# Modulation weights of the first block dealt out unit by unit between the linears of a two-block transformer kernel

## The chip, the cores and the metric

One Trainium2 chip, one of its NeuronCores. The time is that of one execution on the device in microseconds (us); of several executions the median is given. Beside it stands the profile of one execution.

## The reference

Two models run one after the other on 256 tokens of width 1024 (the second also on 256 context tokens), each two layers deep. Only the first matters here:

```python
for l in range(DEPTH):                        # DEPTH = 2
    mod = silu(c) @ w_mod[l] + b_mod[l]       # 1024 -> 6 x 1024, one vector
    sh1, sc1, g1, sh2, sc2, g2 = split(mod, 6)
    h = modulate(rms_norm(x, mix_norm_g[l]), sh1, sc1)
    x = x + g1 * token_mixer(h, ...)
    h = modulate(rms_norm(x, ffn_norm_g[l]), sh2, sc2)
    x = x + g2 * channel_mixer(h, ...)        # up, causal conv of 3 taps, silu(a) * b, down
```

The token mixer has three branches that a gate merges: attention from latents (q and k are expanded from normed latents by `w_uq` and `w_ukv`, head-normed and rotated), attention from a plain projection ("qkb", "vb"), and a gated depthwise convolution of 31 taps ("conv"). The modulation vector of a layer is six groups of 1024 numbers; a group needs 1024 x 1024 weights, 4 MB, for one vector. The second model's layers have nine groups for two vectors.

## The kernel before

**Weights.** All weights lie in one stream in the order of use, cut into units of eight 128x128 blocks (512 KB). SyncE loads unit u into slot u % 8 of `ring` (L499) as soon as TensorE has done with unit u - 8. `weight_blocks` writes the order out by hand; TensorE's code asks for the blocks in the same order.

**Split units.** Large matmuls are made in three passes of a faster format: ScalarE copies a landed unit into `heads` (L1148, four slots), VectorE writes the remainder into `rests` (L1537), and TensorE multiplies head by head, head by rest and rest by head (L577 to L579). Splits are placed into the programs of ScalarE and VectorE by `upcoming` (up to three split units and five units ahead of the unit that an event belongs to) or, in the FFNs, two behind each pair of output blocks. uq, uk, uv, pw2, oa, ob, out and the modulation weights aren't split; their matmuls are at L581, each in two entries of the trace.

**Modulation.** `mod_rows` on TensorE takes a group: unit k holds the weights of input block k for all 1024 outputs, two matmuls with 32 columns as stationary operand and 512 moving ones. They go to output partitions 32 * (2 * (k % 2) + r) for r = 0, 1 of one PSUM bank, so that an even and an odd unit use four different strips of the array. ScalarE copies the bank into `rows` (L1313), `mod_cols` on TensorE turns it into columns with eight entries of 2 or 4 moving columns, and VectorE adds the bias (L1551). A group whose matmuls are put between other work is called a guest.

**Order in a mixer.** lat (six units), guest group 2 as a whole, the squares' sums of the latents (ones-matmuls), uq, uk, uv, `mod_cols` of group 2 and guest group 3 as a whole (`hook`), then `head_norm` of q: for each of four pairs of heads a bank of head sums, behind it one pair of qkb output blocks (two units), then the rotation. `head_norm` of k likewise with the conv blocks. Then vb, `mod_cols` of group 3 and guest group 4 as a whole, the head sums of qkb's keys, three gate pairs (`early_gates`), and attention with five more. VectorE makes for each head pair a reciprocal of 128x512 (L1640) and a product (L1641), for each rotation three operations (L1653 to L1656); ScalarE the root ahead of the reciprocal (L1199, in `roots`). PSUM banks 0 to 5 go round: `take_bank` waits for whoever read the tenant before. ScalarE copies the four qkb banks (L1360, L1362, L1179) behind all four roots of q and the squares of k.

**Order in an FFN of the first block.** 22 pairs j of up-projection blocks, two units each (the first two pairs together as a quad), and behind pairs 3 and 4, 10 and 11, 17 and 18 four guest units each; `mod_cols` behind pairs 5, 12 and 19. Then the down-projection.

Two layers of mixer and FFN make up the first 1260 us or so.

## Time and profile before

| | |
|---|---|
| median of 3 runs | 2936.59 us (2926.67 to 2941.27) |
| profiled execution | 2939.55 us, span 2937.8 us |
| granted TensorE clock, mean | 0.970 of full speed |
| busy: TensorE, its weight loads, VectorE, ScalarE | 94%, 79%, 57%, 37% of the span |
| stream | 836 units of 512 KB, mean 152 GB/s |
| chain that ended last | TensorE 84%, VectorE 8%, DMA 3%, ScalarE 3% |

A row of the trace's timeline has the start, the length, the engine, the line, the tiles written and read, the shape and the number of instructions merged; in brackets the idle time of the engine before it and what ended it. PE is TensorE, DVE VectorE, ACT ScalarE. Ends of matmuls are modelled and overlap the next start a little.

### The profile page before, as it was taken

To read this page: it belongs to the slowest core of one execution; us is meant where nothing else is said; L and a number is where in the kernel's file an instruction comes from. 1 tells how busy PE (TensorE), PEld (TensorE's weight loads), DVE (VectorE), ACT (ScalarE), POOL (GpSimd) and SP (SyncE) were. 2 spreads that over 40 slices of the span, in tenths; PEclk is the share of its full clock that TensorE was granted. 3 is DMA by queue.
4 is the path that set the end of the run, shared out by engine and by line. 5 is a ranking of instruction groups with operands and counts; after the bars stand their busy time and mean duration, and the time that the engine had idled before them with its cause. 6 is when DMAs were issued, how large, how long until landed. Compare 5 with 4: busy or idle time off the path is not lost.

```text
span 2937.8 us, 38582 instructions
## 1 busy us (share of the span) xinstructions
PE 2761.8 (94%) x15792; PEld 2329.9 (79%) x15792; DVE 1661.9 (57%) x2417; ACT 1097.8 (37%) x1660; POOL 51.6 (2%) x54
## 2 busy tenths in 40 slices
PE   7898899998988989989999899999989999989998
PEld 4777788896777988977878784888877788878998
DVE  4689436753896366655555534564565554364554
ACT  3445325643454155533122322222233222234443
POOL 0000000000000000000000000000000000000000
PEclk8999999999999999999999999999999999999999
DMA  8451346656332557536454312444334543231453
GB/s 331 172 172 58 116 156 242 223 160 222 127 120 77 194 196 252 184 123 229 143 186 137 108 64 68 140 147 139 138 129 167 186 156 136 94 101 40 156 185 116
DMA packets 122753, 447.27 MB, mean 152 GB/s; under 512 B 13521, under 2 KB 14929, under 8 KB 122193
## 3 DMA queue, kind: packets, MB, share of 16 engines
q1 hardware_dynamic: 122576, 444.81, 44.3%
q8 instruction: 125, 2.05, 0.3%
q14 instruction: 52, 0.42, 0.0%
HBM read 443.71 MB, written 1.05 MB: 151 GB/s over the span
## 4 chain that ended last, share of the span: by engine, by line
PE 84%; DVE 8%; DMA 3%; ACT 3%; issue 1%; SPq 0%; ACTq 0%; DVEq 0%
PE ps L577 22%; PE ps L578 22%; PE ps L579 22%; PE ps L581 18%; DMA ring<-stream 3%; DVE area L1640 2%; DVE rests L1537 1%; DVE area L1844 1%; DVE rs L1600 1%; ACT heads L1148 1%; DVE area L1610 0%; DVE stat L1672 0%; DVE sg L1684 0%; DVE rt L1736 0%; DVE h_split L1618 0%
## 5 line engine op out<-in xcount | busy, mean ns | idle before, releaser
L577 PE MATMUL ps<-h_split,heads 128*128 128x256 f32 (+1 forms) x2992 | 1006.7, 336 | 99.5 <-DVE h_split L1618 57.2
L578 PE MATMUL ps<-h_split,heads 128*128 128x256 f32 (+1 forms) x2992 | 986.3, 330 | 0.0
L579 PE MATMUL ps<-h_split,rests 128*128 128x256 f32 (+1 forms) x2992 | 985.8, 329 | 0.0
L1537 DVE TENSOR_TENSOR rests<-ring,heads 128x1024 fp32r<-128x1024 f32 x520 | 631.1, 1231 | 362.1 <-ACT heads L1148 354.5
L1148 ACT ACTIVATE heads<-ring 128x1024 fp32r<-128x1024 f32 x520 | 536.9, 1056 | 594.6 <-PE ps L579 298.1
L577 PEld LDWEIGHTS ps<-h_split,heads 128*128 128x128 f32 x2992 | 588.3, 197 | 190.2 <-DVE h_split L1618 62.7
L578 PEld LDWEIGHTS ps<-h_split,heads 128*128 128x128 f32 x2992 | 588.4, 197 | 48.3 <-issue 4.3
L579 PEld LDWEIGHTS ps<-h_split,rests 128*128 128x128 f32 x2992 | 587.1, 196 | 46.1
L577 PE MATMUL ps<-hid_split,heads 128*128 128x256 f32 (+1 forms) x1056 | 355.2, 336 | 0.0
L579 PE MATMUL ps<-hid_split,rests 128*128 128x256 f32 (+1 forms) x1056 | 354.9, 336 | 0.0
L578 PE MATMUL ps<-hid_split,heads 128*128 128x256 f32 (+1 forms) x1056 | 354.9, 336 | 0.0
L1760 DVE TENSOR_TENSOR sg<-sg,ps 128x512 f32<-128x512 f32 (+1 forms) x88 | 54.7, 622 | 330.4 <-PE ps L579 284.6
L581 PE MATMUL ps<-area,ring 128*128 128x256 f32 (+1 forms) x800 | 210.0, 423 | 13.7 <-DVE area L1804 9.8
L1301 ACT ACTIVATE sg<-ps 128x512 f32<-128x512 f32 (+1 forms) x88 | 47.6, 541 | 458.8 <-PE ps L579 458.8
L578 PEld LDWEIGHTS ps<-hid_split,heads 128*128 128x128 f32 x1056 | 199.3, 189 | 20.7
L579 PEld LDWEIGHTS ps<-hid_split,rests 128*128 128x128 f32 x1056 | 199.3, 189 | 20.6
L577 PEld LDWEIGHTS ps<-hid_split,heads 128*128 128x128 f32 x1056 | 199.3, 189 | 20.3
L581 PEld LDWEIGHTS ps<-area,ring 128*128 128x128 f32 x800 | 155.1, 196 | 63.3 <-issue 40.4
L1630 DVE SCALAR_TENSOR_TENSOR x_sb<-ps,mods_sb,x_sb 128x256 f32<-128x256 f32 x160 | 71.9, 480 | 162.3 <-PE ps L581 85.1
L1574 DVE SCALAR_TENSOR_TENSOR qt<-ring,cols,qt 128x1024 f32<-128x1024 f32 x84 | 104.2, 1282 | 57.0 <-DMA ring<-stream 55.9
L1736 DVE SCALAR_TENSOR_TENSOR rt<-work,cols,rt 128x256 f32<-128x256 f32 x176 | 77.5, 482 | 51.3 <-ACT work L1251 49.7
L1844 DVE SCALAR_TENSOR_TENSOR area<-area,cols 128x256 f32<-128x256 f32 x240 | 100.2, 480 | 1.1
(180 smaller groups left out, 2226.1 us busy)
## 6 DMA issues: line engine op xcount, KB each, us to landing
ring<-stream SPq DMA_DIRECT2D x836, 512.0 KB, 3.8
consts<-constants SPq DMA_DIRECT2D x1, 1728.0 KB, 11.0
x_sb<-x_in SPq DMA_DIRECT2D x1, 1024.0 KB, 11.5
x_sb<-ctx_in SPq DMA_DIRECT2D x1, 1024.0 KB, 4.8
out<-area SPq DMA_DIRECT2D x1, 1024.0 KB, 4.8
consts<-constants SPq DMA_DIRECT2D x1, 576.0 KB, 8.9
cols<-columns SPq DMA_DIRECT2D x1, 538.0 KB, 9.9
cols<-columns SPq DMA_DIRECT2D x1, 157.5 KB, 2.4
```

The costliest lines, as they stand in the source:

```text
L577: nc.tensor.matmul(out, lhsT[0], rhs[0], start=first, stop=False)
L578: nc.tensor.matmul(out, lhsT[0], rhs[1], start=False, stop=False)
L579: ins = nc.tensor.matmul(out, lhsT[1], rhs[0], start=False, stop=last)
L581: ins = nc.tensor.matmul(out, lhsT, rhs, start=first, stop=last)
L1148: nc.scalar.activation(heads[:, n % HEADS_RING, :], ring[:, u % RING, :], ACT.Copy)\
L1537: nc.vector.tensor_tensor(rests[:, u % RING, :], ring[:, u % RING, :], as_f32(heads[:, n % HEADS_RING, :]), ALU.subtract)\
L1574: ins = nc.vector.scalar_tensor_tensor(out=half[:, v, :], in0=ring[:, u % RING, :], scalar=c, in1=half[:, v, :], op0=ALU.mult, op1=ALU.add)
L1630: nc.vector.scalar_tensor_tensor(out=x[:, v, m, :], in0=bank((p, *what, m))[:, t], scalar=gate(m, v), in1=x[:, v, m, :], op0=ALU.mult, op1 ...
L1640: step(nc.vector.reciprocal(b, b))
L1736: nc.vector.scalar_tensor_tensor(out=zc[:, s, ab, :], in0=z[:, s, ab, tap:tap + SEQ], scalar=cols[:, at:at + 1], in1=zc[:, s, ab, :], op0= ...
L1760: step(nc.vector.tensor_tensor(s_, s_, src, ALU.mult), (p, "gated", j))
L1844: nc.vector.scalar_tensor_tensor(out=dwc[:, c, :], in0=u_pad[:, c, tap:tap + SEQ], scalar=w, in1=dwc[:, c, :], op0=ALU.mult, op1=ALU.add)\
```

## The change

The eight units of a guest group are dealt out. In the first block's two FFNs each group goes over six successive pairs (units 0 and 1, 2, 3, 4 and 5, 6, 7), `mod_cols` behind the seventh; groups begin at pairs 0, 7 and 14. In a mixer three units of group 2 stand ahead of the latents' ones-matmuls and five behind; group 3 is spread over uq (2), uk (2) and the four qkb pairs (1 each), group 4 over the four conv pairs and the first four gate pairs. `mod_cols` of group 2 comes behind uq and that of group 3 ahead of the second conv pair; that of group 4 stays. ScalarE copies the first two qkb banks between the roots of q, and copies the rows of groups 3 and 4 later in its order. The stream's order follows. VectorE's order changes only with the pairs at which it adds an FFN group's bias. The second model's FFNs keep their places.

```diff
+def mixer_guests(l, stage, c):
+    _, second, third = MIXER_MODS[l]
+    if stage in ("uq", "uk"):
+        return second, [2 * (stage == "uk"), 2 * (stage == "uk") + 1]
+    if stage == "qkb":
+        return second, [4 + c]
+    if stage == "conv":
+        return third, [c]
+    return third, [4 + c] if c < 4 else []
...
+SPREAD = 6
...
 def guest_at(up, j):
     groups = FFN_MODS[up]
-    every = FJ // max(len(groups), 1)
+    if up in ("up_0", "up_1"):
+        q, at = divmod(j, SPREAD + 1)
+        if q < len(groups):
+            return groups[q], [k for k in range(KD) if k * SPREAD // KD == at]
+        return None, []
...
@@ the stream @@
         linear(f"uq_{l}", Q_RANK // P, range(HEADS))
+        guests(l, "uq")
         linear(f"uk_{l}", KV_RANK // P, range(HEADS))
+        guests(l, "uk")
         wide(f"uv_{l}", KV_RANK // P, 4)
-        mods(MIXER_MODS[l][1])
-        linear(f"qkb_{l}", KD, range(HEADS))
-        linear(f"conv_{l}", KD, range(2 * CC))
+        for stage in ("qkb", "conv"):
+            for c in range(4):
+                linear(f"{stage}_{l}", KD, (2 * c, 2 * c + 1))
+                guests(l, stage, c)
         wide(f"vb_{l}", KD, 4)
-        mods(*MIXER_MODS[l][2:])
         for m in range(KD):
             linear(f"gate0_{l}", KD, (m,))
             linear(f"gate1_{l}", KD, (m,))
+            guests(l, "gate", m)
...
@@ TensorE, mixer @@
-                hook(*guests[0])
+                mod_rows(*guests[0], range(3))
                 out = take_bank((p, "latms"))
...
+                mod_rows(*guests[0], range(3, KD))
...
+                mod_cols(*guests[0])
+                guests_behind("uq")
...
+                guests_behind("uk")
...
-                hook(*guests[1])
                 def pair_behind(what, name):
                     def do(c):
+                        if what == "conv" and c == 1:
+                            mod_cols(*guests[1])
                         out = take_bank((p, what, c))
                         linear(out[:, 0:SEQ], name, KD, 2 * c, hx)
                         linear(out[:, SEQ:TOK], name, KD, 2 * c + 1, hx, (p, what, c))
+                        guests_behind(what, c)
...
-                hook(*guests[2])
+                pending.append(guests[2])
...
@@ ScalarE, mixer @@
-                mod_rows(*guests[1])
-                roots((p, "qa"), range(4))
-                squares((p, "ka"), range(4), kt)
-                for c in range(2):
+                def second_copies(c):
                     act.wait_ge(tensor_done, after(T, (p, "qkb", c)))
+                    if c >= 2:
+                        copy_pair(pair_of(bt, c), (p, "qkb", c))
+                        return
...
-                for c in (2, 3):
-                    copy_pair(pair_of(bt, c), (p, "qkb", c))
+                roots((p, "qa"), range(4), between=second_copies)
+                squares((p, "ka"), range(4), kt)
+                second_copies(2)
+                second_copies(3)
+                mod_rows(*guests[1])
...
-                for guest in guests[2:]:
-                    mod_rows(*guest)
...
+                def gates_behind(t):
+                    if t % 3 == 2:
+                        early_gates(3 + t // 3)
+                    if t == 2:
+                        mod_rows(*guests[2])
```

## Rows read from the trace of the kernel before

**Rows 1.** The page: busy time, share of the span, instructions.
```profile
PE 2761.8 (94%) x15792; PEld 2329.9 (79%) x15792; DVE 1661.9 (57%) x2417; ACT 1097.8 (37%) x1660; POOL 51.6 (2%) x54
```
**Rows 2.** Stages of the first mixer: us, busy by engine, clock, DMA share, GB/s.
```profile
54.70:96.90 42.20, 37.31 (x175) 23.98 (x174) 5.95 (x7) 12.92 (x20) 0.00 (x0) 0.92 0.72 263
96.90:175.40 78.50, 66.41 (x423) 57.17 (x424) 73.29 (x64) 40.89 (x50) 0.00 (x0) 0.93 0.41 143
...
217.00:306.00 89.00, 79.76 (x542) 69.05 (x541) 83.91 (x227) 50.21 (x109) 0.00 (x0) 0.96 0.21 66
```
**Rows 3.** TensorE's waits in the first FFN (423 to 645): total, times, longest.
```profile
PE ps L577 <- DVE rests L1537: 7.3, 4, 2.5
...
PE ps L581 <- ACT rows L1313: 3.0, 3, 1.0
```
**Rows 4.** The same in the second FFN (1036 to 1257).
```profile
PE ps L577 <- DVE rests L1537: 6.3, 4, 2.3
...
PE ps L581 <- ACT rows L1313: 3.5, 3, 1.5
```
**Rows 5.** TensorE's timeline: lone unit, runs of eight, first entries behind waits.
```profile
15.38 1.05 PE L581 MATMUL ps<-ring,cols 128*32 128x512 f32 x4 [0.21 <-DMA ring<-stream]
...
54.70 4.63 PE L581 MATMUL ps<-ring,cols 128*32 128x512 f32 x32
...
66.57 13.79 PE L581 MATMUL ps<-area,ring 128*128 128x256 f32 x52 [4.88 <-DVE area L1804]
79.78 6.64 PE L581 MATMUL ps<-area,ring 128*128 128x256 f32 x30
...
90.56 4.42 PE L581 MATMUL ps<-ring,cols 128*32 128x512 f32 x32
94.91 1.98 PE L581 MATMUL ps<-sq,consts 128*128 128x512 f32 x4
...
121.00 0.58 PE L577 MATMUL ps<-h_split,heads 128*128 128x256 f32 x1 [4.49 <-ACT area L1362]
...
184.85 0.95 PE L581 MATMUL ps<-consts,rows 128*128 128x2 f32 x8
185.73 3.79 PE L581 MATMUL ps<-ring,cols 128*32 128x512 f32 x32
193.86 0.36 PE L577 MATMUL ps<-h_split,heads 128*128 128x256 f32 x1 [2.44 <-DVE rests L1537]
...
452.88 0.36 PE L577 MATMUL ps<-h_split,heads 128*128 128x256 f32 x1 [1.43 <-DVE rests L1537]
```
**Rows 6.** TensorE's timeline around a run of four units in an FFN.
```profile
500.00 0.28 PE L579 MATMUL ps<-h_split,rests 128*128 128x256 f32 x1
500.21 1.92 PE L581 MATMUL ps<-ring,cols 128*32 128x512 f32 x16
...
502.28 0.28 PE L578 MATMUL ps<-h_split,heads 128*128 128x256 f32 x1
```
**Rows 7.** VectorE's timeline: first reciprocals of the early and the late head norms.
```profile
102.03 3.35 DVE L1640 RECIPROCAL area<-area 128x512 f32<-128x512 f32 x1
...
197.62 3.35 DVE L1640 RECIPROCAL area<-area 128x512 f32<-128x512 f32 x1 [1.26 <-ACT area L1199]
```
**Rows 8.** ScalarE's timeline ahead of the roots of both head norms.
```profile
90.50 1.91 ACT L1354 ACTIVATE kt<-area 32x2048 f32<-32x2048 f32 x1
97.25 1.06 ACT L1148 ACTIVATE heads<-ring 128x1024 fp32r<-128x1024 f32 x1 [4.84 <-DMA ring<-stream]
98.51 1.06 ACT L1148 ACTIVATE heads<-ring 128x1024 fp32r<-128x1024 f32 x1 [0.20 <-DMA ring<-stream]
...
196.90 1.27 ACT L1199 ACTIVATE area<-ps,cols 128x512 f32<-128x512 f32 x2
```
**Rows 9.** TensorE in two stretches of 5 us: busy, clock, DMA share, GB/s.
```profile
470.00:475.00 5.00, 5.00 (x31) 0.66 0.19 77
475.00:480.00 5.00, 5.00 (x44) 1.00 0.64 212
```

More of the change, by code:

```diff
@@ L103, in guest_at @@
     groups = FFN_MODS[up]
-    every = FJ // max(len(groups), 1)
+    if up in ("up_0", "up_1"):
[3 more added lines that the diff above has]
+        return None, []
     for q, group in enumerate(groups):
-        first = GUEST_PAIRS[q] if up in OWN_MODS else 3 + q * every
+        first = GUEST_PAIRS[q] if up in OWN_MODS else 3 + q * (FJ // len(groups))
         if first <= j < first + 3:
-            return group, j - first
-    return None, None
+            return group, list(range(KD))[(j - first) * (KD // 2):(j - first + 1) * (KD // 2)]
+    return None, []
 def is_own(name):
@@ L183, in mods, with guests @@
                     put(name, k, g * KD + n)
+    def guests(l, stage, c=0):
+        (name, g), ks = mixer_guests(l, stage, c)
+        align(UB)
+        for k in ks:
+            for n in range(KD):
+                put(name, k, g * KD + n)
     def own_(unit):
@@ L200, in ffn @@
                     pair(up, up_order(width), 2 * j)
-                guest, part_ = guest_at(up, j)
-                if guest is not None and part_ < 2:
-                    for k in range(part_ * (KD // 2), (part_ + 1) * (KD // 2)):
-                        for n in range(KD):
-                            put(guest[0], k, guest[1] * KD + n)
+                guest, ks = guest_at(up, j)
+                for k in ks:
+                    for n in range(KD):
+                        put(guest[0], k, guest[1] * KD + n)
                 own_(own_unit(up, ("pair", j)))
@@ L648, in norm, with mod_rows @@
                 return once(lambda k: pe.wait_ge(vector_done, V.at((p, "h", k))))
-            def mod_rows(name, g, half=None):
-                if half != 1:
+            def mod_rows(name, g, ks=range(KD)):
+                if 0 in ks:
                     for q in last_mod:
@@ L657, in mod_rows @@
                     last_mod[:] = [(name, g)]
-                for k in range(KD) if half is None else range(half * KD // 2, (half + 1) * KD // 2):
+                for k in ks:
                     for r in range(2):
@@ L727, in ffn @@
                             pair(j, [take_bank((p, kind, j)) for kind in kinds])
-                        guest, part_ = guest_at(up, j)
-                        if guest is not None and part_ < 2:
-                            mod_rows(*guest, part_)
+                        guest, ks = guest_at(up, j)
+                        if ks:
+                            mod_rows(*guest, ks)
                         elif guest is not None:
@@ L792, in _ @@
             mod_cols("mod1_0", 0)
-            mod_rows("mod1_0", 1, 0)
+            mod_rows("mod1_0", 1, range(KD // 2))
             ready = norm(("b1", 0, "mix"), SEQ, 0)
-            mod_rows("mod1_0", 1, 1)
+            mod_rows("mod1_0", 1, range(KD // 2, KD))
             mod_cols("mod1_0", 1)
@@ L815, in _, with guests_behind @@
                             sq[:, k, :], k in (0, 3), k in (2, 4), (p, "latms") if k == 4 else None)
+                mod_rows(*guests[0], range(3, KD))
+                def guests_behind(stage, c=0):
+                    group, ks = mixer_guests(l, stage, c)
+                    mod_rows(*group, ks)
                 for c in range(4):
@@ L862, in early_gates @@
                     linear(out[:, SEQ:TOK], f"gate1_{l}", KD, m, hx, (p, "g01", m))
+                    guests_behind("gate", m)
                 for c in (2, 3):
@@ L1282, in each_pair @@
                         finish(j)
-                        guest, part_ = guest_at(up, j)
-                        if guest is not None and part_ == 1:
+                        guest, ks = guest_at(up, j)
+                        if KD - 1 in ks:
                             mod_rows(*guest, False)
@@ L1401, in per_query @@
                     return lambda b: rs[:, 16 + HEADS * b + t - HEADS:17 + HEADS * b + t - HEADS]
+                def gates_behind(t):
[3 more added lines that the diff above has]
+                        mod_rows(*guests[2])
                 attention((p, "at"), 16, 2, per_query,
-                          lambda c: attn[:, c, :], lambda t: early_gates(3 + t // 3) if t % 3 == 2 else None)
+                          lambda c: attn[:, c, :], gates_behind)
                 act.wait_ge(vector_done, after(V, (p, "cen")))
@@ L1711, in each_pair @@
                         hidden_rests(p, j, T_, lo)
-                        guest, part_ = guest_at(up, j)
-                        if guest is not None and part_ == 2:
+                        guest, ks = guest_at(up, j)
+                        if guest is not None and not ks:
                             mod_cols(*guest, False)
```

## The prediction, made before the changed kernel was run

> **What bounds the kernel now.** I began with the page's busy times: TensorE is busy 94% of the span, VectorE 57%, ScalarE 37% [rows 1]. So almost every microsecond that can be won is one in which TensorE waits, or runs at the lower of its two clock levels, and every microsecond of matmul that is added counts in full unless it falls into such a wait. Then the table of stages [rows 2], for the first block's first mixer. From 54.7 to 96.9 us VectorE is busy 5.95 of 42.2 us. From 96.9 to 175.4 us it is busy 73.3 of 78.5: this stage (the head norms of q and k, with the qkb and conv linears behind them) is VectorE's. From 217 to 306 us (attention) it is VectorE again, 83.9 of 89. So in a mixer what counts is when VectorE gets its first head norm, and how long it stands still before the late ones, which begin at 197.62 [rows 7]. In the FFNs TensorE is the bound, and the chain of waits there is short: in the first, 7.3 us for the weights' low parts (L1537) and 3.0 us for the copy of a group's rows (L1313) [rows 3]; in the second 6.3 and 3.5 us [rows 4].
>
> Both kinds of wait follow a run of modulation units. Eight units of 512 KB are consumed in 3.8 to 4.4 us (185.73 and 90.56 in [rows 5]), and the eight slots of the ring then refill at DMA's pace: after the run of 90.56 ScalarE gets its first qkb unit at 97.25, 4.84 us after it was free, and the next 1.3 us later [rows 8].
>
> **The price of a run.** This is what the change pays with. The 16 entries of four units take 1.92 us (500.21 in [rows 6]), the 4 entries of a unit alone 1.05 us (15.38 in [rows 5]). Within a unit only two of the four 32-column strips of the array are used, an even and an odd unit run beside each other: so the cost goes by rounds, (1.92 - 1.05) = 0.87 us each, and a lone unit pays for a whole round. With the change-over from and to full-width matmuls: from 500.00 to 502.28 are 2.28 us, where two pitches of 5.00/44 = 0.11 us [rows 9] would stand, so two rounds cost 2.06 us net [rows 6], one round alone 2.06 - 0.87 = 1.19 us.
>
> The Trainium skill's page "TensorEngine Tiling (Array Packing)", section Key Properties, says that a change of tiling mode drains TensorE. The rows show this as the 0.14 us between 2.06 and 1.92 for a run; the change makes many more of them. The same page's table under Theoretical Speedup gives a dimension of up to 32 a factor of 4; read for each matmul by itself, a lone unit would cost a quarter of 1.92 us. The row at 15.38 speaks against that reading.
>
> **The FFNs.** The three groups of each FFN go from two runs of four units to six runs of one round (units 0,1 | 2 | 3 | 4,5 | 6 | 7 behind successive pairs). Per group 6 x 1.19 - 2 x 2.06 = +3.0 us, per FFN +9.1 us, all on TensorE. What it buys: waits of 10.3 and 9.8 us. At 7 us of matmuls a pair now meets three or four units of DMA, which at 1.3 us each is 4 to 5 us: the ring stays ahead, and ScalarE no longer stands in front of an unlanded unit. The first wait of 1.43 us (452.88) I keep: it comes from the backlog of the first two pairs, whose results arrive together. The rows' copy then has a pair's time before the pick matmuls and should be hidden; if it isn't, 3 us stay. Bounds of what goes: from 4 us to all. The low clock behind these waits costs 5.00 - 31 x 5.00/44 = 1.5 us a time [rows 9]; one such stretch less in each FFN. First: -8.9 + 9.1 - 1.5 = -1.3 us; second -8.4 + 9.1 - 1.5 = -0.8 us. Ends: +5 and -5 us each.
>
> **The mixers,** by the first.
> (a) Group 2 used to stand ahead of the latents' norm as a run of 4.6 us (54.70). Now three units (two rounds, 2.0) stand there, and the last square of the latents is done by then. The ones-matmuls begin 4.6 - 2.0 = 2.6 us earlier, and with them ScalarE's root, VectorE's reciprocal and the 4.88 us wait at 66.57. The other five units (three rounds, 2.9 us) fill that wait, of which 2 us are left. The low clock behind it costs 13.79 - 52 x 0.221 = 2.3 us, 0.221 being the later pace (6.64 us for 30, at 79.78); I count half of it back, 1.1. Ends 0 and 2.3.
> (b) Group 3's run ahead of the head norms (90.56 to 94.91, 4.35 us) becomes two runs of one round, 2.4. With (a) the first head-norm matmul comes 2.6 + 1.1 + 2.0 = 5.7 us earlier, at 89.2.
> (c) VectorE's first reciprocal stood at 102.03 [rows 7], 7.1 us behind that matmul (94.91 in [rows 5]): ScalarE waited for DMA, copied three units, VectorE split them, and only then came the root. In the new order of units the first qkb units follow uv directly, their slots are freed during uq and uk, and their splitting happens before. What is left ahead of the root is ScalarE's copy of the shared key (1.91 us, till about 91.9) and the root, 0.7. Reciprocal at 92.6, 9.4 us earlier. A split that slips in costs 1.2.
> (d) The loop of eight turns: VectorE takes 175.4 - 102.0 = 73.4 us, 9.2 a turn. TensorE needs 48 x 0.114 [rows 9] and two head matmuls (1.98 at 94.91), 7.5, and with one unit behind each pair 8.6. That leaves it little. The copies of the qkb banks between the roots free the third pair's bank before TensorE comes to it, so the 4.49 us wait at 121.00 and the low clock behind it go; that gives TensorE the room. The two copies of a bank lie ahead of a root whose bank matmul comes only behind the same pair, so they can delay it by their own length, 1.3 us (the length that two roots have at [rows 8]); VectorE is then still at the turn before. I let the loop take as long as now: 9.4 stays. Ends: if each turn grows by its lone unit, 8 x 1.19 = 9.5 are lost; if what VectorE isn't busy of the stage (5.2 us, part of it before 102.03) shrinks, 2 more are won.
> (e) Between vb and the late head norms the pick matmuls (184.85, 0.9) and a run of 3.8 us (185.73) are gone: 9.4 + 0.9 + 3.8 = 14.1. The wait of 2.44 at 193.86, for units that had been issued behind that run, goes: 16.5 at the first gates. VectorE's reciprocal at 197.62 comes earlier by more than that, for ScalarE's root stood behind the late units and the rows' copy, so it isn't the bound. The three gates ahead of attention carry a lone unit each: -3.6. Attention starts 12.9 us earlier; its own unit (1.2) and the rows' copy (0.6) lie beside VectorE's taps. 13 us per mixer, 26 for two. Ends 4 and 18 each.
>
> Nothing behind attention changes, the stream keeps its number of units, and the second model's FFNs keep their order.
>
> **Sum:** -26 - 1.3 - 0.8 = -28 us against the profiled execution's 2939.55; that is 3 us above the median of the runs, so 2936.59 - 28 = 2908.5, say 2908 us.
>
> **Rivals.**
> A. *TensorE becomes the pace of the loop.* The 26 more rounds in all cost 22.6 us and the changes of width some more. For it: 8.6 against 9.2 us a turn, with waits in both directions in every turn. Against: TensorE starts the loop ahead of VectorE. It costs 9.5 us per mixer: gain 28 - 19 = 9, 2928 us.
> B. *Slower: the fetch-ahead gets too short.* Eight slots hold guests too, so that the stream reaches only some two and a half pairs ahead; if ScalarE finds the unit unlanded behind every lone unit, each of the 36 runs in the FFNs brings its own wait. Place: L577 behind a run. At the 1.4 us of 452.88 each they cost 50 us against 28 won: +22, 2959 us. It decides from 43/36 = 1.2 us a run on. Against: today's bursts put eight units into one pair's time, the new order three or four in a pair.
> C. *A lone unit costs a quarter of four,* 0.5 us: 12 rounds in the FFNs and some in the mixers cheaper, 12 us more: 2896 us. The same time comes if every wait and low-clock stretch goes.
> D. *The units were hidden anyway:* the bank wait at 121.00 is VectorE's backlog in another guise, and the last transfer before attention sets the start as now. Against: DMA moves 143 GB/s in the loop and 263 before it [rows 2], so there is room for the units there. Then only (a) and (b) stay, 5.7 us a mixer, and the lone units ahead of attention take 3.6 back: 2 x 2.1 = 4 us, 2932.
>
> **Chances and range.** Forecast (18 to 36 us won) 0.60; C 0.10; A 0.20, half of it beyond 0.5%; D 0.04; B 0.06. A measurement of this kernel tells about 0.5%, 14.7 us, from no change. Faster by more: 0.60 + 0.10 + 0.10 = 0.80; within 0.14; slower 0.06. Range: the forecast and C's near end, A's time below it: 2890 to 2930 us; B is left out, and the far tails of C and D.
>
> **What would show it.** The wait ahead of uq 2 us instead of 4.88; VectorE's first head-norm reciprocal 7 us or more before 102, that of the late heads 14 us or more before 197; no wait on L1362; runs of one unit at 1.05 us; waits for low parts in the FFNs under 2 us each with 9 us more of busy TensorE. Wrong if the loop's turns exceed 10 us, if waits for low parts stand behind lone units, or if the runs of one unit last 0.5 us.

## The result, and the profile after

The changed kernel takes 2896.02 us in the median of 4 runs (2892.64 to 2899.98), the kernel before, measured beside it, 2934.64 us (2926.67 to 2941.27). The ratio is 0.9871, with a 95% interval of 0.9856 to 0.9887: 37.9 us less, between 33.2 and 42.3. Forecast were 28 us less, 2908 us; the range of 2890 to 2930 holds the result.

The page's busy times of the profiled execution (2896.45 us, span 2894.6), to be laid beside [rows 1]:

```profile
PE 2772.1 (96%) x15792; PEld 2314.3 (80%) x15792; DVE 1661.0 (57%) x2417; ACT 1098.8 (38%) x1660; POOL 51.6 (2%) x54
```

The same number of matmuls keeps TensorE busy 10.3 us longer, in a span that is 43.2 us shorter. So 53.5 us in which it did nothing are gone. (The execution profiled of before was one of its slower ones, 5 us above its median. The difference of the medians is the result; the profiles show where it lies, and their stages add up to 5 us too much.)

The span cut at the same instructions of both timelines: TensorE's first matmul of each mixer, of each FFN and of the second model, and its first matmul on attention's values.

| stretch | before | after | change | forecast |
|---|---|---|---|---|
| to the first mixer | 34.63 | 33.89 | -0.7 | 0 |
| first mixer up to attention's values | 189.14 | 170.96 | -18.2 | -13 |
| from there to the first FFN | 199.92 | 199.91 | 0.0 | 0 |
| first FFN | 229.07 | 224.33 | -4.7 | -1.3 |
| second mixer up to attention's values | 188.28 | 168.86 | -19.4 | -13 |
| from there to the second FFN | 195.00 | 197.37 | +2.4 | 0 |
| second FFN | 231.64 | 228.94 | -2.7 | -0.8 |
| second model | 1670.1 | 1670.3 | +0.2 | 0 |

The gain is where it was forecast, in the two mixers ahead of attention and a little in the FFNs, and larger in each of the four. Up to attention's values TensorE stands still for 6.2 us in each mixer (170.96 us less 164.74 busy in the first), before for 23.3 and 21.9. Its busy time there fell by 1.1 and 3.7 us, though six rounds were added: the mean granted clock rose from 0.93 and 0.92 to 0.98 and 0.99.

TensorE's timeline of the first mixer after the change; rows of split matmuls are left out except the first behind the only wait in the loop and the first of the gates:

```profile
53.46 1.91 PE L611 MATMUL ps<-ring,cols 128*32 128x512 f32 x12
55.30 2.43 PE L611 MATMUL ps<-sq,consts 128*128 128x256 f32 x10
57.66 2.77 PE L611 MATMUL ps<-ring,cols 128*32 128x512 f32 x20
62.61 12.28 PE L611 MATMUL ps<-area,ring 128*128 128x256 f32 x48 [2.18 <-DVE area L1855]
...
88.23 1.88 PE L611 MATMUL ps<-sq,consts 128*128 128x512 f32 x4
95.78 1.05 PE L611 MATMUL ps<-ring,cols 128*32 128x512 f32 x4
...
104.43 1.05 PE L611 MATMUL ps<-ring,cols 128*32 128x512 f32 x4
...
118.59 0.39 PE L607 MATMUL ps<-h_split,heads 128*128 128x256 f32 x1 [0.54 <-DVE rests L1588]
...
171.90 1.88 PE L611 MATMUL ps<-sq,consts 128*128 128x512 f32 x4
173.21 0.68 PE L607 MATMUL ps<-h_split,heads 128*128 128x256 f32 x1
...
179.45 1.05 PE L611 MATMUL ps<-ring,cols 128*32 128x512 f32 x4
```

Against [rows 5]: the wait ahead of uq is 2.18 instead of 4.88 us, the lone units run 1.05 us, the 4.49 us wait on the bank's copy and the 2.44 us ahead of the first gates are gone. A turn of the loop takes TensorE 104.43 - 95.78 = 8.65 us. The stages of the same mixer, in the columns of [rows 2]:

```profile
53.46:90.30 36.84, 34.66 (x162) 23.23 (x162) 9.62 (x10) 15.25 (x23) 0.00 (x0) 0.95 0.84 304
90.30:162.50 72.20, 71.66 (x462) 55.62 (x461) 69.22 (x61) 38.73 (x48) 0.00 (x0) 1.00 0.57 183
198.00:287.00 89.00, 79.54 (x546) 68.01 (x545) 82.95 (x226) 49.41 (x109) 0.00 (x0) 0.98 0.23 78
```

In the loop TensorE is now busy 71.66 of 72.20 us, VectorE 69.22: before they had 66.41 and 73.29 of 78.50. The granted clock of the stretch rose from 0.93 to 1.00. VectorE's reciprocals of the first mixer, to [rows 7]:

```profile
91.71 3.35 DVE L1691 RECIPROCAL area<-area 128x512 f32<-128x512 f32 x1 [5.11 <-ACT area L1240]
...
113.13 3.35 DVE L1691 RECIPROCAL area<-area 128x512 f32<-128x512 f32 x1
126.45 3.35 DVE L1691 RECIPROCAL area<-area 128x512 f32<-128x512 f32 x1
...
148.79 3.35 DVE L1691 RECIPROCAL area<-area 128x512 f32<-128x512 f32 x1
174.73 3.35 DVE L1691 RECIPROCAL area<-area 128x512 f32<-128x512 f32 x1 [2.75 <-ACT area L1240]
```

The first is 10.3 us earlier than before, the first of the late heads 22.9. Last, the FFNs: waits of TensorE in the first and in the second, to [rows 3, 4].

```profile
PE ps L607 <- DVE rests L1588: 0.8, 1, 0.8
```
```profile
PE ps L607 <- DVE rests L1588: 1.7, 1, 1.7
```

One wait for low parts is left in each, and none for the rows' copy.

### The profile page after: what moved, and what is told of

Read it like the earlier page. It is cut to its first block, busy times and chain, and to the rows that moved or that the text cites. A ratio compares the mean times of both kernels' runs of the same rounds, so it can differ in the third digit from the quotient of the medians.

```text
span 2894.6 us, 38586 instructions
## 1 busy us (share of the span) xinstructions
PE 2772.1 (96%) x15792; PEld 2314.3 (80%) x15792; DVE 1661.0 (57%) x2417; ACT 1098.8 (38%) x1660; POOL 51.6 (2%) x54
## 3 DMA queue, kind: packets, MB, share of 16 engines
HBM read 443.71 MB, written 1.05 MB: 154 GB/s over the span
## 4 chain that ended last, share of the span: by engine, by line
PE 89%; DVE 6%; ACT 2%; DMA 1%; issue 1%; SPq 0%; DVEq 0%; ACTq 0%
PE ps L607 23%; PE ps L608 23%; PE ps L609 23%; PE ps L611 20%; DMA ring<-stream 1%; DVE area L1691 1%; DVE rs L1651 1%; DVE rests L1588 1%; DVE area L1895 1%; DVE area L1661 0%; DVE sg L1735 0%; DVE stat L1723 0%; ACT heads L1189 0%; DVE h_split L1669 0%; DVE rs L1851 0%
## 5 line engine op out<-in xcount | busy, mean ns | idle before, releaser
L607 PE MATMUL ps<-h_split,heads 128*128 128x256 f32 (+1 forms) x2992 | 1002.0, 335 | 61.3 <-DVE h_split L1669 57.1
L607 PEld LDWEIGHTS ps<-h_split,heads 128*128 128x128 f32 x2992 | 580.0, 194 | 164.7 <-DVE h_split L1669 62.7
L608 PEld LDWEIGHTS ps<-h_split,heads 128*128 128x128 f32 x2992 | 580.4, 194 | 49.7 <-issue 5.3
L609 PEld LDWEIGHTS ps<-h_split,rests 128*128 128x128 f32 x2992 | 579.3, 194 | 46.1
L611 PE MATMUL ps<-ring,cols 128*32 128x512 f32 x608 | 112.5, 621 | 6.9 <-DMA ring<-stream 6.7
## 6 DMA issues: line engine op xcount, KB each, us to landing
consts<-constants SPq DMA_DIRECT2D x1, 1728.0 KB, 10.9
x_sb<-x_in SPq DMA_DIRECT2D x1, 1024.0 KB, 11.2
cols<-columns SPq DMA_DIRECT2D x1, 538.0 KB, 10.1
```

The lines of the kernel that those rows point to most:

```text
L607: nc.tensor.matmul(out, lhsT[0], rhs[0], start=first, stop=False)
L608: nc.tensor.matmul(out, lhsT[0], rhs[1], start=False, stop=False)
L609: ins = nc.tensor.matmul(out, lhsT[1], rhs[0], start=False, stop=last)
L611: ins = nc.tensor.matmul(out, lhsT, rhs, start=first, stop=last)
```

## The experiments

Two explanations of the 10 us above the forecast were open. One is that single terms of the sum had the wrong size: what the lone unit costs, how many stretches of low clock go, how long the loop over the head pairs takes. The other, rival C, is that a lone unit costs less than a round. And one assumption behind the loop's term was not tested by the result: that VectorE sets its pace. Each kernel below was timed in five rounds beside the kernel before. The difference in us is the ratio less one times the median of before, as measured beside it. An interval is some 4 to 6 us wide to either side, so that two of these kernels are told apart only from about 7 us on. Below that the timelines must decide, and each of them is of one execution, whose stages can differ by some us without an edit (last section).

| kernel | ratio to before | interval | difference, us |
|---|---|---|---|
| the change | 0.9871 | 0.9856 to 0.9887 | -37.9 |
| ffn_only | 0.9975 | 0.9963 to 0.9987 | -7.3 |
| mixers_only | 0.9880 | 0.9861 to 0.9899 | -35.2 |
| copies_only | 0.9971 | 0.9957 to 0.9985 | -8.5 |
| no_copies_between | 0.9922 | 0.9905 to 0.9939 | -22.9 |
| latents_behind | 0.9896 | 0.9877 to 0.9915 | -30.5 |
| loop_two | 0.9881 | 0.9861 to 0.9900 | -34.9 |
| loop_two_no_copies | 0.9899 | 0.9885 to 0.9912 | -29.7 |
| ffn_two | 0.9839 | 0.9817 to 0.9861 | -47.2 |
| ffn_two_early | 0.9851 | 0.9838 to 0.9865 | -43.7 |
| gates_late | 0.9865 | 0.9844 to 0.9886 | -39.6 |
| gates_late_two | 0.9843 | 0.9830 to 0.9857 | -46.1 |
| all_two | 0.9830 | 0.9816 to 0.9843 | -49.9 |

### The two halves alone

**ffn_only**: the kernel before with the FFNs of the change.

```diff
 def guest_at(up, j):
+    if up in ("up_0", "up_1"):
+        q, at = divmod(j, SPREAD + 1)
+        if q < len(groups):
+            return groups[q], [k for k in range(KD) if k * SPREAD // KD == at]
+        return None, []
```

> Only the two FFNs of the first block deal their groups out over six pairs; stream and order of the mixers are those of before. Theory M (the gains read off the two traces stage by stage add up, and each stage keeps its own): first FFN -4.7 us, second -2.7, together -7 us against before; the low parts' waits fall to under 2 us each, TensorE is 8 to 9 us busier in each FFN at equal clock, and two stretches of low clock per FFN are missing (1.7 us each). The prediction's own sum: -2 us. Rival S: the FFNs profit only because the mixers in front of them end with the ring fuller, then 0 or slower by some us.

**mixers_only**: the changed kernel with the FFNs of before.

```diff
 def guest_at(up, j):
-    if up in ("up_0", "up_1"):
-        q, at = divmod(j, SPREAD + 1)
-        if q < len(groups):
-            return groups[q], [k for k in range(KD) if k * SPREAD // KD == at]
-        return None, []
```

> The mixers as in the changed kernel, the FFNs' groups in runs of four units as before. Theory M: -35 us against before (18 and 17 us for the two mixers). The prediction's own sum: -26 us. With M, this gain and that of the FFNs alone add up to the whole change within 3 us.

Measured: -7.3 us (3.8 to 10.9) and -35.2 us (29.6 to 40.8). Theory M had -7 and -35, the prediction's sum -2 and -26; rival S is out. Together they are 42.5 us, the whole change 37.9, within the intervals. So the halves add up, and both were forecast too small: by some 5 us and some 9. (The two excesses add up to more than the whole's 10 us; the intervals allow for that.)

The FFN's part in windows (busy time by engine, clock, DMA share, GB/s): first the kernel before, from 440 to 647 us and from 1053 to 1258 us, behind the low clock with which each FFN begins, and in them four stretches of 5 us.

```profile
440.00:647.00 207.00, 195.77 (x1595) 185.37 (x1593) 134.52 (x206) 116.05 (x182) 3.70 (x5) 0.98 0.64 218
1053.00:1258.00 205.00, 194.95 (x1584) 184.02 (x1582) 134.88 (x204) 115.84 (x180) 6.47 (x5) 0.98 0.64 219
470.00:475.00 5.00, 5.00 (x31) 5.00 (x31) 4.66 (x8) 2.86 (x5) 0.00 (x0) 0.66 0.19 77
569.00:574.00 5.00, 5.00 (x31) 5.00 (x31) 4.44 (x7) 3.08 (x5) 0.00 (x0) 0.66 0.18 71
1081.00:1086.00 5.00, 5.00 (x31) 5.00 (x31) 4.49 (x8) 3.02 (x5) 0.00 (x0) 0.66 0.39 148
1180.00:1185.00 5.00, 5.00 (x31) 5.00 (x31) 4.20 (x7) 3.33 (x6) 0.00 (x0) 0.66 0.15 59
```

Then the same of the changed kernel, and of ffn_only's first FFN.

```profile
421.00:623.40 202.40, 200.58 (x1598) 184.60 (x1598) 134.21 (x206) 116.73 (x182) 3.71 (x5) 1.00 0.69 224
1012.00:1214.60 202.60, 200.55 (x1596) 184.13 (x1594) 135.30 (x205) 117.62 (x181) 6.47 (x5) 1.00 0.68 222
```
```profile
432.00:635.00 203.00, 201.64 (x1606) 184.81 (x1600) 134.95 (x207) 117.43 (x183) 3.72 (x5) 1.00 0.67 224
```

Before, two places in the first FFN run for a while at the lower clock level, 470 and 569 us, each behind a pair of waits (1.20 and 0.97 us; 2.17 and 0.99), and so do two in the second, 1081 and 1180 us (0.62 and 0.99; 2.30 and 1.47). The middle pair of waits of each FFN (2.47 and 1.02; 1.92 and 1.02) is followed by none. A mean clock of 0.66 over 5 us is 1.7 us lost, so each FFN lost 3.4 us in these places; the forecast had counted one of them per FFN, at 1.5 us. In both FFNs of the changed kernel and in the first of ffn_only the mean of the stretch is 1.00. The second FFN of ffn_only still has one such place, behind its wait of 1.91 us, and a mean of 0.99.

### What a lone unit costs

**ffn_two**: the FFNs' groups go in twos. The aim is the price of a round, and a faster kernel if that price holds.

```diff
 SPREAD = 6
+TWO_BEHIND = (0, 2, 4, 5)
...
         q, at = divmod(j, SPREAD + 1)
-        if q < len(groups):
-            return groups[q], [k for k in range(KD) if k * SPREAD // KD == at]
+        if q < len(groups) and at == SPREAD:
+            return groups[q], []
+        if q < len(groups) and at in TWO_BEHIND:
+            first = 2 * TWO_BEHIND.index(at)
+            return groups[q], [first, first + 1]
```

> The changed kernel, but the FFNs' groups go in four runs of an even and an odd unit (behind the pairs 0, 2, 4 and 5 of a group's seven) instead of six runs, two of two units and four of one. Theory R (a run is paid by rounds, and a lone unit pays a whole one): two rounds with their changes of width less per group, 2 x 1.15 = 2.3 us, 7 us per FFN, 14 us faster than the changed kernel (about -51 against before), provided that no wait for low parts comes back; a run of two units lasts 1.05 us like one of one. Rival C (a lone unit costs a half or a quarter of two): 0 to -3 us. Rival W (two guest units at a time outrun the ring): waits for low parts of over 1 us behind the runs, less than 7 us won.

Measured: 2885.45 us, -47.2 us against before, 9 us faster than the change by the ratios. TensorE's timeline in its first FFN:

```profile
424.10 1.07 PE L615 MATMUL ps<-ring,cols 128*32 128x512 f32 x8
433.76 0.35 PE L611 MATMUL ps<-h_split,heads 128*128 128x256 f32 x1 [2.65 <-DVE rests L1592]
439.67 1.06 PE L615 MATMUL ps<-ring,cols 128*32 128x512 f32 x8
```

Eight entries, an even and an odd unit, last 1.06 us; four entries, a lone unit, 1.05 us (above). That is theory R, and rival C's price is refuted, in the prediction and here: a lone unit pays the whole round. The Trainium skill's page "TensorEngine Tiling (Array Packing)", section Key Properties, says that different tiles of the array work independently of each other; the two rows agree: two units beside each other take no longer than one. A lone unit has no neighbour to profit from that. In windows, the first FFN of ffn_two up to the end of its down-projection is 210.54 us of busy TensorE; that of the changed kernel, below it, 216.82:

```profile
402.86:617.10 214.24, 210.54 (x1706) 198.22 (x1706) 142.86 (x224) 124.34 (x194) 3.71 (x5) 0.99 0.65 220
```
```profile
404.76:623.40 218.64, 216.82 (x1706) 199.25 (x1706) 142.63 (x224) 124.34 (x194) 3.71 (x5) 0.99 0.66 215
```

6.28 us for six runs fewer: a run of one round costs 1.05 us in the FFN, not the 1.19 of the prediction (the second FFN gives 6.28 us as well). The wait behind the third pair is longer, 2.65 against 0.77 us in the first FFN and 2.57 against 1.72 in the second; that is what is missing from 2 x 6.3 us: the two FFNs are 4.4 and 5.4 us shorter. Half of rival W came true.

**ffn_two_early**: the first group of each FFN in twos behind pairs 0 to 3, to fill that wait.

```diff
-TWO_BEHIND = (0, 2, 4, 5)
+TWO_BEHIND = ((0, 1, 2, 3), (0, 2, 4, 5))     # first group, the other two
```

> Like ffn_two, but the first of an FFN's three groups has its four runs of two units behind pairs 0 to 3 instead of 0, 2, 4 and 5. In the changed kernel and in ffn_two the first pair behind pair 3 starts 30.9 us after the FFN's first matmul whether four rounds of guests stand ahead of it or two, so VectorE's backlog sets it and rounds ahead of it cost nothing: the wait of 2.6 us shrinks to about 0.6 and 1 to 2 us an FFN are won, 2 to 4 us faster than ffn_two (about -52 against before). Rival: with eight guest units ahead of pair 4 its own units land too late (ten units and eight guests in some 31 us), and the wait grows by 1 us or more.

Measured: 2891.89 us, -43.7 us, 3.5 slower than ffn_two by the ratios (their intervals overlap). The timeline decides:

```profile
435.71 0.36 PE L611 MATMUL ps<-h_split,heads 128*128 128x256 f32 x1 [4.44 <-DVE rests L1592]
```

The wait grew from 2.65 to 4.44 us, and the second FFN shows the same, 4.43. The FFNs are 2.9 and 3.7 us longer than ffn_two's, more than the 1.8 and 1.9 us by which the wait grew. More of each FFN runs at the low clock; how much of the rest that is was not separated. The FFN had begun at 400.95, so the pair begins 34.8 us behind it, not 30.9. My reading that VectorE's backlog fixed that moment is refuted: with eight guest units ahead of the pair its own units are late. The rival had it. That the transfers are what makes them late is the rival's reading; the row shows only that the wait is for the units' low parts.

### Who sets the pace of the loop

**copies_only**: the kernel before, with ScalarE's copies of the first two qkb banks between the roots.

```diff
-                roots((p, "qa"), range(4))
-                squares((p, "ka"), range(4), kt)
-                for c in range(2):
-                    ...                        # wait, copy, square of bank c
+                roots((p, "qa"), range(4), between=second_copies)
+                squares((p, "ka"), range(4), kt)
```

> The kernel before with one thing changed: ScalarE copies the first two qkb banks between the roots of q. Stream and TensorE's order are those of before. Theory V (VectorE sets the loop's pace, TensorE's wait of 4.49 us on the copy matters only through the 2.0 us that VectorE then stands still between q's and k's head norms): the wait goes and the time falls by 2.0 to 2.3 us a mixer, 4 to 5 in all. Rival T (TensorE sets the pace): the 4.49 us wait and the low clock behind it (2 us) come back in full, 13 us in all. Rival Z (the copies delay the roots): 0 or slower by up to 3 us.

**no_copies_between**: the changed kernel with these copies put back.

```diff
-                roots((p, "qa"), range(4), between=second_copies)
+                roots((p, "qa"), range(4))
                 squares((p, "ka"), range(4), kt)
+                second_copies(0)
+                second_copies(1)
```

> The changed kernel with the first two qkb copies put back behind all four roots of q and the squares of k. Theory T (with a lone unit behind each pair TensorE sets the loop's pace at 8.64 us a turn, so that whatever it waits is lost): TensorE stands about 4.4 us ahead of the third qkb pair and runs at the low clock behind, 6 to 8 us a mixer, 12 to 16 us slower than the changed kernel (about -24 against before). Rival V (VectorE, at 8.62 to 9.09 us a turn, sets it): 2.3 us a mixer, 5 us slower than the changed kernel (about -34 against before).

Measured: copies_only -8.5 us against before (4.4 to 12.6), V's 4 to 5 at the edge of the interval, T's 13 just outside. In its profiled execution the mixers are 6.4 and 5.2 us shorter up to attention's values. Of that, 2.7 and 1.1 us lie ahead of the first reciprocal, where the edit changes nothing, 2.2 and 2.6 are the pause between q's and k's head norms, and 1.4 and 1.6 lie behind the eighth reciprocal. So the edit is worth 3.7 and 4.2 us, 8 in all: the pause that V counted, and a part behind the loop, where I take it that TensorE, no longer held up, comes sooner (no row shows that link by itself). no_copies_between is 15 us slower than the change, as T had it; V's 5 is out. VectorE's fourth and fifth reciprocal show both. Before, with the wait for TensorE that lies between them:

```profile
123.45 3.35 DVE L1640 RECIPROCAL area<-area 128x512 f32<-128x512 f32 x1
136.66 0.69 DVE L1653 TENSOR_TENSOR rt<-ps,sin_a 128x512 f32<-128x512 f32 x1 [1.36 <-PE ps L581]
139.09 3.35 DVE L1640 RECIPROCAL area<-area 128x512 f32<-128x512 f32 x1
```

In copies_only:

```profile
120.87 3.35 DVE L1642 RECIPROCAL area<-area 128x512 f32<-128x512 f32 x1
134.28 3.35 DVE L1642 RECIPROCAL area<-area 128x512 f32<-128x512 f32 x1
```

In no_copies_between, with TensorE's wait that lies between them:

```profile
111.34 3.35 DVE L1693 RECIPROCAL area<-area 128x512 f32<-128x512 f32 x1
130.91 3.35 DVE L1693 RECIPROCAL area<-area 128x512 f32<-128x512 f32 x1
```
```profile
110.09 0.58 PE L607 MATMUL ps<-h_split,heads 128*128 128x256 f32 x1 [4.49 <-ACT area L1405]
```

From the fourth to the fifth are 15.64 us before (123.45 and 139.09), 13.41 in copies_only, 13.32 in the changed kernel (113.13 and 126.45), 19.57 here. All other distances of the eight are equal in these kernels, 4.2, 8.6 and 9.1 us. The wait is 4.49 us in both kernels that have it. So the same wait costs VectorE 2.2 us a mixer where TensorE has no guest units in the loop, and 6.2 us where it has one behind each pair: there TensorE has no room to make up the wait and the low clock behind it (0.63 in the mean from 110 to 118 us). Up to attention's values the second mixer is 6.4 us longer than in the changed kernel, the first 3.9 (it came to its first reciprocal 2.4 us sooner, with less low clock ahead of it). The rest of the 15 us has nothing to do with the copies: in this kernel's profiled execution the two stretches behind attention are 1.0 and 3.6 us longer, and the second FFN 1.7.

**loop_two**: the lone units of the loop in twos behind every second pair, so that TensorE has half the rounds of guests there.

```diff
     if stage == "qkb":
-        return second, [4 + c]
+        return second, [3 + c, 4 + c] if c % 2 else []
     if stage == "conv":
-        return third, [c]
+        return third, [c - 1, c] if c % 2 else []
```

> The changed kernel, but in the loop over head pairs the guest units stand in twos behind every second pair (four runs instead of eight a mixer). Theory T (TensorE alone sets the loop's pace): 4 rounds of 1.1 us a mixer come back, 9 us faster in all. Theory B (both engines stand close to each other: TensorE 8.64 us a turn, VectorE 8.62 and 9.09): TensorE then waits for VectorE's splits instead, 0 to 2 us a mixer, at most 4 in all.

**loop_two_no_copies**: both edits.

> loop_two (guest units in twos behind every second pair of the loop) with the two qkb copies back behind the roots. Theory B (TensorE and VectorE stand close to each other in the loop; putting the copies back cost the changed kernel 15 us because TensorE had no room to catch up the wait of 4.49 us and the low clock behind it): with 4.4 us less of TensorE's work in the loop it catches up a part, and the copies are worth what they were worth in the kernel before, 7 us: 7 us slower than loop_two, about -28 against before. Rival T (TensorE alone sets the pace): 13 us or more slower than loop_two, -22 or less against before.

Measured: loop_two -34.9 us, 3 slower than the change and not told apart from it. That is theory B; T's 9 us faster is out. Its timeline has three waits for low parts in the first loop:

```profile
102.55 0.39 PE L607 MATMUL ps<-h_split,heads 128*128 128x256 f32 x1 [0.53 <-DVE rests L1588]
...
119.79 0.39 PE L607 MATMUL ps<-h_split,heads 128*128 128x256 f32 x1 [1.72 <-DVE rests L1588]
...
155.45 0.39 PE L607 MATMUL ps<-h_split,heads 128*128 128x256 f32 x1 [2.21 <-DVE rests L1588]
```

The 4.4 us that TensorE was given (four rounds at 1.1, an estimate) came back as 4.5 us of waits for VectorE, where the changed kernel has 0.54. From the first to the eighth reciprocal VectorE waits for nothing in either kernel, and both take 57.1 us. So VectorE does set the pace, as the prediction had it, and TensorE with a lone unit behind each pair has half a microsecond to spare in the whole loop. loop_two_no_copies has -29.7 us, 5 slower than loop_two (7 expected by B, 13 or more by T). From the fourth to the fifth reciprocal it has 18.48 us:

```profile
114.91 3.35 DVE L1693 RECIPROCAL area<-area 128x512 f32<-128x512 f32 x1
133.39 3.35 DVE L1693 RECIPROCAL area<-area 128x512 f32<-128x512 f32 x1
```

That is 5.2 us more than in loop_two, nearly as much as the 6.2 of no_copies_between, but up to attention's values the two mixers are only 3.8 and 3.6 us longer than in loop_two: 1.5 us of it is made up behind the eighth reciprocal, by a TensorE that has room. In no_copies_between nothing is made up there. Theory T is refuted as a rule for the loop; what it had right is that the change used up the slack.

### The latents' norm

**latents_behind**: all eight units of group 2 ahead of the ones-matmuls.

```diff
-                mod_rows(*guests[0], range(3))
+                mod_rows(*guests[0])
...
-                mod_rows(*guests[0], range(3, KD))
```

> The changed kernel, but all eight units of group 2 stand ahead of the latents' ones-matmuls as before. Expected by the prediction's step (a): the ones-matmuls and all that hangs on them come 2.7 us later, the wait ahead of uq grows from 2.2 to 4.9 us, and up to 1.1 us of low clock come with it: 2.7 to 3.8 us a mixer, 5 to 8 us slower than the changed kernel. Rival: the head norms wait for something else (the splits of the first qkb units), and then less than 2 us in all.

Measured: -30.5 us, 7.4 slower than the change and within the 5 to 8 that step (a) gave. By the times alone the rival's 2 us would not be quite out; in the timelines the mixers are 2.3 and 4.1 us longer up to attention's values, all of it ahead of the first reciprocal. The wait ahead of uq is the old one:

```profile
65.23 0.76 PE L611 MATMUL ps<-area,ring 128*128 128x256 f32 x1 [4.88 <-DVE area L1854]
```

### The units ahead of attention

**gates_late**: the last four units of group 4 behind gate pairs 3 to 6, in attention.

```diff
-    return third, [4 + c] if c < 4 else []
+    return third, [1 + c] if 3 <= c < 7 else []
...
-                    if t == 2:
+                    if t == 11:
                         mod_rows(*guests[2])
```

> The changed kernel, but the last four units of group 4 stand behind gate pairs 3 to 6, all within attention, instead of 0 to 3, of which three stand ahead of attention; the rows' copy follows. If TensorE sets the time up to attention and VectorE in it, three lone runs with their changes, 3 x 1.1 = 3.3 us a mixer, go from the path: 6 to 7 us faster than the changed kernel. Rival: attention's TensorE, 90% busy, hands the runs' time on: 0, or some us slower.

**gates_late_two**: in two runs, behind gate pairs 3 and 4.

```diff
-    return third, [4 + c] if c < 4 else []
+    return third, [2 * c - 2, 2 * c - 1] if c in (3, 4) else []
...
-                    if t == 2:
+                    if t == 5:
                         mod_rows(*guests[2])
```

> The changed kernel with the last four units of group 4 in two runs of an even and an odd unit, behind gate pairs 3 and 4 in attention. Theory G (what gates_late won ahead of attention, 5.7 and 3.6 us, was given back by four lone runs among attention's matmuls): two rounds less there, 2 us a mixer come back, 4 to 6 us faster than the changed kernel. Rival P (it was given back by the low clock's place and a longer first wait in the second FFN, which have nothing to do with the runs): within 2 us of the changed kernel, as gates_late.

Measured: -39.6 and -46.1 us, against -37.9 of the change. In both timelines attention's values come 165.2 or 165.1 us behind the first mixer's start instead of 170.96, and 165.3 us instead of 168.86 in the second: 5.8 and 3.6 us less. In the first mixer some 2.2 us of it lie ahead of the first reciprocal, where no edit is; gates_late's comes 55.6 us behind the mixer's start, the changed kernel's 57.8:

```profile
90.84 3.35 DVE L1691 RECIPROCAL area<-area 128x512 f32<-128x512 f32 x1 [4.56 <-ACT area L1240]
```

That leaves 3.5 and 3.6 us for the three lone units, 1.2 each, and this is step (e)'s price. In gates_late the two attentions together hand back 3.4 us; in windows, from the first values to the last:

```profile
200.45:285.37 84.92, 77.74 (x534) 64.02 (x535) 78.25 (x212) 48.00 (x104) 0.00 (x0) 0.99 0.26 88
790.84:878.39 87.55, 81.46 (x534) 67.64 (x535) 78.25 (x212) 48.01 (x104) 0.00 (x0) 0.95 0.25 85
```

They were 83.71 and 85.37 us in the changed kernel. Another 3.0 us are lost in the second FFN, whose first wait is 3.18 us instead of 1.72. gates_late_two has 86.10 us in the second attention, 1.45 less, and by the ratios it is 6.5 us faster than gates_late (4.4 by the medians), which fits theory G; but the intervals overlap, and its second FFN too begins with a longer wait (2.88 us). How much of the difference is the two rounds and how much rival P's clock is left open.

### Together

**all_two**: ffn_two_early, gates_late_two, and two units instead of three ahead of the latents' ones-matmuls.

> ffn_two_early, gates_late_two and two units of group 2 instead of three ahead of the latents' ones-matmuls (a round of 0.9 us moves into the wait ahead of uq). If the parts add up: -12 to -14 us for the FFNs, 0 to -6 for the gates, -1 for the latents, against the changed kernel: 2875 to 2883 us, about -55 against before. Rival: the parts share the same slack, and no more than ffn_two's 2885 comes out.

Measured: 2887.05 us, -49.9 us (46.1 to 54.0): the lowest ratio of all, though not the lowest median, and 12 us (by the ratios) faster than the change, but not told apart from ffn_two. The forecast of -55, or 2875 to 2883 us, was missed, and the rival's "no more than ffn_two" can't be told from what came. It carries ffn_two_early's wait (4.43 us in both FFNs). A kernel with ffn_two's order in the FFNs and gates_late_two's in the mixers should stand at some 2880 us by these parts (an estimate: 2896 less 9 and 8); it wasn't run.

## Why the prediction was right, and where it was too small

**What bounds the kernel.** Right: the gain is in waits and in clock, and the added busy time of TensorE counts in full except where it falls into a wait (loop_two: some 4.4 us less work, no gain).

**The price of a run.** The step "a lone unit pays for a whole round" is shown (1.05 us for one unit, 1.06 for two). The size, 1.19 us net for one round, was 0.14 too high in the FFNs: six runs cost 6.28 us in ffn_two. There the change of width costs nothing that can be seen. Ahead of attention it was right: three lone units cost 3.5 us in gates_late, 1.18 each. The prediction read the 0.14 us of [rows 6] as the price of the drain of which the Trainium skill's page "TensorEngine Tiling (Array Packing)" speaks in section Key Properties, and these runs show a price of 0.13 us a run in one place and none in the other; what makes the difference is open.

**FFNs.** The waits: -9.4 and -8.0 us (the part of the windows in which TensorE isn't busy went from 11.2 to 1.8 and from 10.1 to 2.1 us) against -8.9 and -8.4. The low clock: two stretches less in each FFN, 3.4 us, where the term had one, 1.5 us. This is the term that was mis-sized most. The busy time: +4.7 and +5.3 us, which is the runs less the clock. With the clock added back (3.4 us in the first; 2.8 in the second, where the low clock of the FFN's start took 0.6 us more than before) the runs cost 8.1 us in each, an estimate, against 9.1. Sum -4.7 and -2.7 against -1.3 and -0.8, and -7.3 for both against -2 by ffn_only. The place of rival B shows no wait behind a lone unit but one in each FFN.

**Mixers.** By the first, the forecast in parentheses, and with the 1.24 us taken off by which its guest group began earlier: (a) the ones-matmuls 2.7 us earlier (2.6), the wait 2.18 (2). (b) The head norm 5.4 us earlier (5.7). (c) VectorE's first reciprocal 9.1 us earlier (9.4); VectorE now waits 5.11 us for ScalarE's root, that is, nothing slipped in. (d) Here the prediction was off by size: "I let the loop take as long as now". From the first reciprocal to the eighth it takes 57.1 us instead of 59.4. (The far end of the step's range, "2 more are won", is what came.) The 2.3 us are the pause between q's and k's head norms in which VectorE waited for TensorE, which itself had waited 4.49 us on the copy. I had named that wait as TensorE's alone and counted no time for it on VectorE's side. copies_only shows it by itself, and with what is saved behind the loop it is the largest term that was missing: 8.5 us over both mixers (4.4 to 12.6). (e) The run and the pick matmuls ahead of the late heads: 4.6 us (4.7). The stop ahead of the first gates: 3.1 us (2.44), and the 48 matmuls behind it take 6.3 us where the low clock had made 7.5 of them. From the first gates to attention's values are 31.6 us instead of 29.9: the three lone units cost 3.5 us (gates_late; 3.6), and a stretch of low clock that went with the stop gives back 1.8 that the sum did not have. Added up: 9.1 + 2.6 + 4.6 + 3.1 - 1.7 = 17.7 us instead of 13 (2.6 being (d) up to TensorE's start of vb), 18.2 with 0.5 won in lat, the six units ahead of the guest group; and 19.4 in the second mixer. The 2.4 us lost behind attention there are the clock's place (last section).

**Rivals.** A didn't come: the turn is 8.65 us, but VectorE's, too. It may have been nearer than its chance of 0.20 says: TensorE is busy 71.66 of 72.20 us, and one wait put back costs 6.2 us at VectorE instead of 2.2. B came as one wait in each FFN, not as 36, and as 4.4 us in ffn_two_early. C's price is refuted; its other condition, that waits and low-clock stretches go, came nearly true, and its 2896 us is the result. That the two numbers agree so well is luck: C counted 12 cheaper rounds in the FFNs, where the order has 24 lone units. D is refuted by the mixers' gain.

## What to carry to other kernels

When a burst of work that lies between other stages is dealt out, price it by what it is paid in (here rounds of the array, not units), and deal it in the smallest portions that are whole: two units, even and odd, cost what one does (it paid in the FFNs, not in the loop, where VectorE sets the pace). When a wait goes, look also at what other engine stood still because of it, and at the clock behind it: both were missing here, and made up most of the 10 us. And a stretch in which two engines run at the same pace has no slack: here an edit that freed TensorE won nothing (loop_two), while one that delayed it by 4.49 us cost VectorE 6.2 us a mixer (no_copies_between). A delay of VectorE wasn't tried.

## What the runs showed of the hardware that was not expected

The clock's place moves time between executions and between layers. The same 66 matmuls behind attention, in the two layers of one execution of the changed kernel (windows: length, busy by engine, clock, DMA share, GB/s):

```profile
288.56:307.28 18.72, 14.28 (x66) 11.96 (x66) 4.37 (x4) 7.09 (x11) 0.00 (x0) 0.74 0.03 12
883.32:897.84 14.52, 10.00 (x66) 8.75 (x66) 4.37 (x4) 7.09 (x11) 0.00 (x0) 1.00 0.07 23
```

18.72 us at a mean granted clock of 0.74 (between the levels of 1.2 and 2.4 GHz), 14.52 at 1.00; gates_late has 15.8 in the second layer. Such a difference of 4 us is no effect of an edit. The same shows between executions: from attention's first values to the first FFN the kernel before and ffn_only have the same instructions in the same order.

```profile
223.77:423.69 199.92, 183.41 (x1078) 161.08 (x1079) 118.35 (x272) 75.25 (x145) 3.64 (x5) 0.95 0.35 111
222.35:417.31 194.96, 175.96 (x1078) 154.97 (x1079) 118.36 (x272) 75.36 (x144) 3.64 (x5) 0.99 0.34 114
```

The 5 us between them are the clock's (TensorE is busy 7.5 us longer for the same work, and a part of that falls into its waits), and over the profiles of all kernels here this stretch takes 194.9 to 201.8 us. The stretch from a mixer's start to its first reciprocal moves too: 55.4 to 58.5 us in the kernels whose order there is that of the change, 63.6 to 67.4 in those whose order there is that of before. So a stage of one profile must not be read more finely than 3 to 5 us, and the 9.1 us of (c), read from one pair of profiles, is no surer than that. In the loop of the changed kernel and in its FFNs, behind the low clock with which each begins, almost no wait was left, and the mean clock was 1.00.
